# Joined entries and stage changes: tile order at three entries, the last weight slab of the delta layer, key squares, values and the first output tile

## The chip, the cores and the metric

The kernel runs on one core of a Trainium2 chip. The metric is the device time of one execution in microseconds (us), the median of the timed runs. Lower is better. TensorE is called PE here, VectorE DVE, ScalarE ACT, GpSimd POOL and SyncE SP.

## The reference

A block of three layers on 512 tokens of width 1024, all in float32: a bidirectional gated delta layer (8 heads) with its MLP, a bidirectional gated linear attention layer (4 heads) with its MLP, and a modulated layer with latent attention (4 heads, 256 context tokens ahead of the 512) beside four pooling groups.

```python
for i in range(2):
    m = _mixer_gdn(x, ...) if i == 0 else _mixer_gla(x, ...)
    x = _layernorm(DEEPNORM_ALPHA * x + m, ln1_g[i], ln1_b[i])
    x = _layernorm(DEEPNORM_ALPHA * x + _sq_relu_mlp(x, mlp_w1[i], mlp_w2[i]), ln2_g[i], ln2_b[i])
# second block
q, k, v = _mla_qkv(u, ...); kc, vc = ...      # q, k: rms-normed over 128 + 64 rotary columns
attn = _attend(q, concat(kc, k), concat(vc, v))
y = _branches(u, attn, w_pool, pool_scale) @ w_out
x = x + gate[:, None, :] * y
```

`_mixer_gdn` projects x to q, k, v, z and gates, convolves, and solves per head a triangular system in chunks; the kernel does that by doubling in levels.

## The kernel before

**Weights.** Every large product takes its weights in slabs of 1 MB (128 partitions x 2048 columns) through two raw halves. `load_slab` (L239, SP queue) fetches a half when the low part of the one before it is made. `split_hi` (L247, ACT) rounds a half to the high part `whi`, `split_lo` (L255, DVE) subtracts to the low part `wlo`, and `mm3` (L278, lines 280 to 282, PE) multiplies high by high, high by low and low by high. A slab is therefore two ACT and two DVE instructions of 1024 columns each. The semaphores `w_hi_ready` and `w_ready` count the halves in the order of the slabs, so the order of the splits is fixed while their place in each engine's program is free.

**Engines and order.** Each engine has its own program, written out by hand; engines meet only at semaphores. An instruction waits behind all that stand ahead of it on its own engine.

**The entries.** A token stage (a_out, down0, b_out) ends with x of 4 tiles of 128 tokens. `dve_token_end` (L487) adds and normalizes each tile (`dve_norm_tile` L431: sum, statistics, then after ACT's `act_norm_tile` two instructions, in two halves each for tile 3), PE turns it (`pe_turn_half`), ACT's `act_turned` makes its high parts `act_hi` and `dve_turned` (L416) its low parts `act_lo`, two halves for a tile. Before, DVE makes tile 1's low parts between tile 3's statistics and tile 3's norm. `pe_feature_first` (L1582) opens the next feature stage (up0, b_qk, up1): it needs tiles 0 and 1 to begin, multiplies them for output tiles 0 and 1 in groups of three matmuls of 256 columns, turns the two halves of tile 3 after the first and the second four groups of output tile 0, and goes on with tiles 2 and 3.

**The delta layer.** `pe_a_in` projects in 16 slabs. Behind the last one ACT and DVE split the second slab of a_out (`next_pair("a_in", 7)`, b = 1) and then begin the heads: a table load, `act_a_decays`, `act_a_decay(0)` (L1256), DVE's `dve_a_k` and `dve_a_first_pairs` (L1374, L1380), and PE's `pe_a_decay_turn` (L1023). Each of the 8 heads has levels l = 1 to 6, each with products (L1092), transposes (L1101), copies on ACT and products and additions on DVE (L1440, L1453).

**c_in and attention.** `pe_c_in` ends with head 0's keys, their sums, the query sums (L2608) and six value products (L2583), alternating between banks 6 and 7, read out by ACT (t = 0, 2, 4) and DVE (t = 1, 3, 5). ACT and DVE split the second slab of c_out ahead of these. `pe_c_attend` goes through 16 steps n, four query tiles for each of four heads. A step has the next tile's score (L2834, L2835, banks 0 to 3), pieces of the next head's preparation (key products L2600, query L2590, sums L2604, L2608, in bank 7), the value product of the step before (L2854, bank 6) and the transposes of the probabilities (L2843, banks 4 and 5). DVE's `dve_c_softmax`, `dve_c_max`, `dve_c_rope` (L2759) and `dve_c_keys` (L2764, L2765) belong to it; the last two scale the next head's key and rotary key by its norm, in the step with qt = 2. GpSimd adds the rotary squares and does the pooling beside it. At the end `act_c_mix` and `dve_mix` (L570, L574) split the mixed tiles and c_out begins.

## Time and profile before

| | |
|---|---|
| timed runs | median 1873.69 us (1873.48 to 1875.39, 3 runs) |
| profiled execution | 1872.41 us, its span 1870.4 us |
| PE busy | 1820.5 us, 97% of the span |
| DVE busy | 986.4 us, 53% |
| ACT busy | 733.7 us, 39% |
| POOL busy | 235.6 us, 13% |
| split_hi, one half (L253) | 1053 ns, 214 times |
| split_lo, one half (L259) | 1224 ns, 214 times |
| granted clock, mean | 0.993 of full speed |

Busy times are those of the profile's first part, the two splits those of its fifth. The span runs from the first to the last instruction; the rest of the execution lies around it. The granted clock is TensorE's; 1.00 is 2.4 GHz.

### The profile page before, as it was taken

The page shows a single profiled execution, that of the slowest core. Times are in us where ns is not written, and L with a number is a line of the kernel's source. Part 1 is how long each engine was busy: PE and PEld are TensorE (multiplying, and loading weights), DVE is VectorE, ACT ScalarE, POOL GpSimd, SP SyncE. Part 2 cuts the span into 40 slices and gives each one's busy share as a digit, 9 for nine tenths or more (in the row PEclk, how much of TensorE's full clock was granted, in tenths as well). Part 3 has the DMA queues.
Part 4 walks back from the last instruction along what each step waited for, and adds up shares of the span by engine and source line. Part 5 has one row for each costly group of instructions (what it writes and reads, how often), then busy time and mean ns, then how long its engine had stood idle before and what let it go on. Part 6 is the DMA issues. An engine that isn't in the chain of part 4 may idle for free.

```text
span 1870.4 us, 24188 instructions
## 1 busy us (share of the span) xinstructions
PE 1820.5 (97%) x9152; PEld 1471.2 (79%) x9152; DVE 986.4 (53%) x1393; ACT 733.7 (39%) x1209; POOL 235.6 (13%) x230
## 2 busy tenths in 40 slices
PE   8999999999999999999999999999999998999999
PEld 6887798888788888887777787888888887875667
DVE  5775466666554453356321577744443567323663
ACT  4344455554232232333443444222223355334340
POOL 2001234342000001000000253000000000201500
PEclk9999999999999999999999999999999999999999
DMA  5323100000342234222222200442235222421001
GB/s 157 90 90 112 46 2 1 1 1 1 122 148 90 90 90 149 90 90 90 68 91 68 68 1 23 129 164 90 90 112 180 90 90 79 149 70 45 1 1 68
DMA packets 102374, 146.77 MB, mean 78 GB/s; under 512 B 4977, under 2 KB 70721, under 8 KB 102032
## 3 DMA queue, kind: packets, MB, share of 16 engines
q1 hardware_dynamic: 95472, 121.45, 20.5%
q0 software_dynamic: 6816, 24.13, 3.9%
q8 instruction: 59, 0.97, 0.2%
q14 instruction: 27, 0.22, 0.0%
HBM read 143.47 MB, written 2.10 MB: 78 GB/s over the span
## 4 chain that ended last, share of the span: by engine, by line
PE 91%; DVE 3%; issue 2%; ACT 2%; POOL 1%; DMA 1%; SPq 0%; ACTq 0%; DVEq 0%; POOLq 0%
PE bk L280 23%; PE bk L282 23%; PE bk L281 23%; PE bk L1092 2%; PE bk L1110 2%; PE bk L2834 1%; PE bk L2835 1%; PE bk L1101 1%; PE bk L2854 1%; PE bk L990 1%; POOL work L1512 1%; PE bk L1973 1%; PE bk L1008 1%; PE bk L1121 1%; PE bk L1152 1%
## 5 line engine op out<-in xcount | busy, mean ns | idle before, releaser
L259 DVE TENSOR_TENSOR wlo<-raw,whi 128x1024 fp32r<-128x1024 f32 x214 | 253.4, 1224 | 376.9 <-ACT whi L253 373.2
L280 PE MATMUL bk<-act_hi,whi 128*128 128x512 f32 x960 | 384.0, 400 | 0.3 <-DVE wlo L723 0.3
L281 PE MATMUL bk<-act_lo,whi 128*128 128x512 f32 x960 | 380.6, 396 | 0.0
L282 PE MATMUL bk<-act_hi,wlo 128*128 128x512 f32 x960 | 380.5, 396 | 0.0
L253 ACT ACTIVATE whi<-raw 128x1024 fp32r<-128x1024 f32 x214 | 216.1, 1053 | 265.5 <-PE bk L282 248.8
L280 PE MATMUL bk<-whi,act_hi 128*128 128x512 f32 x768 | 308.6, 402 | 2.5 <-DVE act_lo L473 1.8
L281 PE MATMUL bk<-wlo,act_hi 128*128 128x512 f32 x768 | 304.8, 397 | 0.0
L282 PE MATMUL bk<-whi,act_lo 128*128 128x512 f32 x768 | 304.7, 397 | 0.0
L280 PEld LDWEIGHTS bk<-act_hi,whi 128*128 128x128 f32 x960 | 180.5, 188 | 48.9 <-issue 4.1
L282 PEld LDWEIGHTS bk<-act_hi,wlo 128*128 128x128 f32 x960 | 180.5, 188 | 44.5
L281 PEld LDWEIGHTS bk<-act_lo,whi 128*128 128x128 f32 x960 | 180.6, 188 | 44.4 <-issue 1.0
L280 PEld LDWEIGHTS bk<-whi,act_hi 128*128 128x128 f32 x768 | 145.5, 189 | 38.9 <-issue 3.1
L282 PEld LDWEIGHTS bk<-whi,act_lo 128*128 128x128 f32 x768 | 145.3, 189 | 36.1
L281 PEld LDWEIGHTS bk<-wlo,act_hi 128*128 128x128 f32 x768 | 145.4, 189 | 34.6 <-issue 0.5
L1633 DVE TENSOR_TENSOR arena<-arena (+1 forms) x64 | 44.3, 692 | 182.2 <-ACT arena L1616 182.2
L1616 ACT ACTIVATE arena<-bk 128x512 f32 (+1 forms) x64 | 38.3, 598 | 245.2 <-PE bk L282 245.2
L1942 POOL TENSOR_TENSOR work<-work,arena 128x512 f32<-128x512 f32 x24 | 37.5, 1583 | 381.3 <-ACT work L1926 355.5
L473 DVE TENSOR_TENSOR act_lo<-arena,act_hi 128x2048 fp32r<-128x2048 f32 x32 | 73.3, 2292 | 18.8 <-ACT act_hi L467 18.8
L829 DVE SCALAR_TENSOR_TENSOR work<-work,convw 128x512 f32<-128x512 f32 x96 | 64.6, 743 | 0.0
L467 ACT ACTIVATE act_hi<-arena 128x2048 fp32r (+1 forms) x32 | 60.9, 1904 | 6.3 <-PE bk L282 6.3
L1092 PE MATMUL bk<-work 128*128 128x128 f32 x384 | 61.1, 280 | 1.3 <-DVE work L1433 1.2
L1440 DVE TENSOR_TENSOR work<-bk,work 128x256 f32<-128x256 f32 x96 | 40.6, 424 | 36.5 <-PE bk L1092 34.9
(392 smaller groups left out, 2500.8 us busy)
## 6 DMA issues: line engine op xcount, KB each, us to landing
raw<-in_mlp_w SPq DMA_DIRECT2D x128, 512.0 KB, 4.2
raw<-in_a_w_in SPq DMA_DIRECT2D x32, 512.0 KB, 4.0
work<-in_w_mod POOLq DMA_DIRECT2D x24, 512.0 KB, 4.1
raw<-in_b_w_in SPq DMA_DIRECT2D x24, 512.0 KB, 3.8
raw<-in_w_in SPq DMA_DIRECT2D x14, 512.0 KB, 4.0
raw<-in_a_w_out SPq DMA_DIRECT2D x8, 512.0 KB, 4.2
raw<-in_b_w_out SPq DMA_DIRECT2D x8, 512.0 KB, 4.0
raw<-in_w_out SPq DMA_DIRECT2D x8, 512.0 KB, 3.9
```

Of the source, the lines that this page charges most:

```text
L253: nc.scalar.activation(whi[b][:, hs], raw[hf][:, :], ACT.Copy).then_inc(w_hi_ready, 1)
L259: nc.vector.tensor_tensor(wlo[b][:, hs], raw[hf][:, :], whi[b][:, hs], ALU.subtract).then_inc(w_ready, 1)
L280: nc.tensor.matmul(acc, lhs_hi, rhs_hi, start=first, stop=False, skip_group_check=True)
L281: nc.tensor.matmul(acc, lhs_hi, rhs_lo, start=False, stop=False, skip_group_check=True)
L282: return nc.tensor.matmul(acc, lhs_lo, rhs_hi, start=False, stop=last, skip_group_check=True)
L467: nc.scalar.activation(stage(act_hi, b), hid_group(pair, b), ACT.Copy).then_inc(stage_hi_ready, 1)
L473: nc.vector.tensor_tensor(stage(act_lo, b), hid_group(pair, b), stage(act_hi, b), ALU.subtract).then_inc(stage_ready, 1)
L829: nc.vector.scalar_tensor_tensor(out=acc, in0=src, scalar=wk, in1=acc, op0=ALU.mult, op1=ALU.add).then_inc(conv_step, 1)
L1092: mm = nc.tensor.matmul(bk[s][:, c % 2 * P:c % 2 * P + P], A["K"][:, c, :], z_right(l, c * P, P), start=True, stop=True, skip_group_check= ...
L1440: nc.vector.tensor_tensor(A["T"][:, 2 * s:2 * s + 2, :], chunks(bk[s])[:, 0:2, :], A["negpair"][:, l, :].unsqueeze(1).broadcast_to([P, 2, ...
L1616: nc.scalar.activation(head_tile(hid, k2 * 4, 2 * b + j), bk[2 * b + j][:, :], ACT.Relu).then_inc(acc_free, 1)
L1633: nc.vector.tensor_tensor(tile, tile, tile, ALU.mult).then_inc(hid_ready, 1)
```

## The change

- Entries: DVE makes tile 1's low parts ahead of tile 3's sum, and tile 2's low parts one half ahead of tile 3's norm and one behind it. ACT makes tile 2's high parts ahead of tile 3's statistics. PE turns the two halves of tile 3 after the first and second four groups of output tile 1.
- Delta layer: the last slab is split in the heads h = 1 and h = 2 (the second and third), one half in each, behind level 3.
- c_in: the six value products go to banks 2, 3, 6, 7, 4, 5, each with the wait for that bank's reader; the waits for their copies move behind the first score.
- Attention: the second slab of c_out is split one half at n = 3 and one at n = 7. Head 1's second key product goes to bank 6 and doesn't wait for the first one's square. The keys of the next head are scaled ahead of the softmax of qt = 2, their rotary part where it was.
- c_out: the first output tile's products of the first slab are issued ahead of the last value product.

```diff
-        def split_hi(act, k, b):
-            for hf in range(2):
+        def split_hi(act, k, b, parts=(0, 1)):
+            for hf in parts:
...
 act_token_end:
-            for st in range(1, ST):
+            for st in (1, 2):
                 act_norm_tile(act, e, st)
                 act_turned(act, e, [st - 1])
+            act_turned(act, e, [2])
+            act_norm_tile(act, e, 3)
             act_turned(act, e, [3])
 dve_token_end:
-            dve_norm_tile(dve, name, e, 3, lambda: dve_turned(dve, e, 1))
-            dve_turned(dve, e, 2)
+            dve_turned(dve, e, 1)
+            dve_norm_tile(dve, name, e, 3, lambda: dve_turned(dve, e, 2, (0,)))
+            dve_turned(dve, e, 2, (1,))
             dve_turned(dve, e, 3)
 pe_feature_first:
                 part(0, range(4 * hf, 4 * hf + 4), 0, 2)
+            for hf in range(2):
+                part(1, range(4 * hf, 4 * hf + 4), 0, 2)
                 pe_turn_half(pe, e, before, 3, hf)
-            part(1, range(0, 8), 0, 2)
 act_a_in (dve_a_in alike):
-                    split_hi(act, next_pair("a_in", k2), b)
+                    if (k2, b) != (7, 1):
+                        split_hi(act, next_pair("a_in", k2), b)
 act_a_head (dve_a_head alike):
+                if l == 3 and h in (1, 2):
+                    split_hi(act, next_pair("a_in", 7), 1, (h - 1,))
 pe_c_in:
-            pe.wait_ge(V.sem, V.at("qt", 0))
-            pe.wait_ge(K.sem, K.at("lnq", 0))
             for t in range(6):
-                if t in (2, 4):
-                    pe.wait_ge(K.sem, K.at("v", t // 2 - 1))
-                if t in (3, 5):
-                    pe.wait_ge(V.sem, V.at("v", t // 2 - 1))
-                T.inc(nc.tensor.matmul(bk[6 + t % 2][:, :]...
+                if t == 0:
+                    pe.wait_ge(acc_free, 2 * FS["c_in"] + 16)
+                elif t == 2:
+                    pe.wait_ge(V.sem, V.at("qt", 0))
+                elif t == 3:
+                    pe.wait_ge(K.sem, K.at("lnq", 0))
+                elif t == 4:
+                    pe.wait_ge(K.sem, K.at("lnk", 1))
+                T.inc(nc.tensor.matmul(bk[V_BANK[t]][:, :]...
-            pe.wait_ge(K.sem, K.at("v", 2))
-            pe.wait_ge(V.sem, V.at("v", 2))
+        V_BANK = (2, 3, 6, 7, 4, 5)
 act_c_in (dve_c_in alike):
-            split_hi(act, next_pair("c_in", 3), 1)
 pe_c_value:
+            elif qt == 0:
+                pe.wait_ge(K.sem, K.at("sqk", 3))
 pe_c_attend:
+                if n == 0:
+                    pe.wait_ge(K.sem, K.at("v", 0))
+                    pe.wait_ge(V.sem, V.at("v", 0))
                 if n + 1 < NB:
                     pe_c_score(pe, n + 1)
+                if n == 0:
+                    pe.wait_ge(K.sem, K.at("v", 2))
+                    pe.wait_ge(V.sem, V.at("v", 2))
...
                 if g < NH and qt == 0:
-                    pe.wait_ge(K.sem, K.at("sqk", 2 * g))
-                    pe_c_key(pe, g, 1, 7)
+                    if g == 1:
+                        pe_c_key(pe, g, 1, 6)
+                    else:
+                        pe.wait_ge(K.sem, K.at("sqk", 2 * g))
+                        pe_c_key(pe, g, 1, 7)
...
                 pe_c_transpose(pe, n)
+                if n == NB - 1:
+                    pe_token_slab(pe, "c_out", 0, 0, 0, 0, True, False, tiles=(0,))
 act_c_attend (dve_c_attend alike):
+                if n in (3, 7):
+                    split_hi(act, next_pair("c_in", 3), 1, (n // ST,))
 dve_c_attend:
+                if qt == 2 and g < NH:
+                    dve_c_key_scaled(dve, g)
                 dve_c_softmax(dve, n)
...
                 if qt == 2 and g < NH:
                     dve_c_rope(dve, g, 7)
-                    dve_c_keys(dve, g)
+                    dve_c_key_rope(dve, g)
```

## Rows read from the trace of the kernel before

**Rows 1.** Waits of PE: engine, line, waited for: us in total, times, longest.

```profile
PE bk L280 <- issue: 5.9, 3, 2.1
```

**Rows 2.** Timeline, up0's entry: start, us, engine, line, tiles, count [idle before <-releaser].

```profile
513.00 1.28 DVE L450 SCALAR_TENSOR_TENSOR X<-X,rstd,work 128x1024 f32<-128x1024 f32 x1
...
514.34 1.09 PE L395 MATMUL bk<-eye,X 128*128 128x128 f32 x8
...
515.91 1.23 DVE L420 TENSOR_TENSOR act_lo<-bk,act_hi 128x512 fp32r<-128x512 f32 x2
...
517.25 0.36 PE L280 MATMUL bk<-act_hi,first_hi 128*128 128x256 f32 x1 [1.82 <-issue]
...
518.75 0.60 PE L395 MATMUL bk<-eye,X 128*128 128x128 f32 x4
...
519.29 0.75 DVE L450 SCALAR_TENSOR_TENSOR X<-X,rstd,work 128x512 f32<-128x512 f32 x1
```

**Rows 3.** Timeline, from the last slab of a_in to the first head.

```profile
204.09 1.99 ACT L253 ACTIVATE whi<-raw 128x1024 fp32r<-128x1024 f32 x2
...
205.24 1.88 PE L1008 MATMUL bk<-work 128*128 128x512 f32 x4
206.10 1.28 ACT L744 ACT_TABLE_LOAD   x1
...
207.93 0.63 ACT L1256 ACTIVATE work<-bk 128x512 f32<-128x512 f32 x1
...
210.03 0.63 PE L1023 MATMUL bk<-eye,work 128*128 128x128 f32 x4 [2.47 <-DVE work L1380]
```

**Rows 4.** Timeline, second head behind level 3, and last head at its level 3.

```profile
251.44 0.87 DVE L1453 TENSOR_TENSOR work<-work,bk 128x256 f32<-128x256 f32 x2 [0.60 <-PE bk L1110]
...
253.68 0.42 DVE L1440 TENSOR_TENSOR work<-bk,work 128x256 f32<-128x256 f32 x1 [1.37 <-PE bk L1092]
...
444.22 1.06 DVE L574 TENSOR_TENSOR act_lo<-act_f,act_hi 128x512 fp32r<-128x512 f32 x1
```

**Rows 5.** Timeline of PE from the end of c_in to the first query tile.

```profile
1699.73 0.95 PE L2608 MATMUL bk<-ones,arena 128*128 128x2 f32 x8
...
1709.97 1.10 PE L2834 MATMUL bk<-work,arena 128*128 128x512 f32 x2 [0.83 <-issue]
...
1717.40 0.70 PE L2600 MATMUL bk<-arena,work 128*128 128x256 f32 x2 [1.18 <-ACT work L2636]
...
1718.85 1.98 PE L2590 MATMUL bk<-arena,work 128*128 128x512 f32 x4
...
1720.67 1.02 PE L2834 MATMUL bk<-work,arena 128*128 128x512 f32 x2
```

**Rows 6.** Timeline, first change of head in attention.

```profile
1732.36 1.57 DVE L2764 TENSOR_TENSOR work<-work 128x768 f32<-128x768 f32 x1
...
1733.86 2.01 DVE L2765 TENSOR_TENSOR work<-arena,work 128x768 f32<-128x768 f32 x1
...
1736.13 2.04 PE L2834 MATMUL bk<-work 128*128 128x512 f32 x2 [1.86 <-DVE work L2765]
...
1743.70 1.02 PE L2834 MATMUL bk<-work 128*128 128x512 f32 x2
```

**Rows 7.** Windows: us; busy of PE, PEld, DVE, ACT, POOL; clock; DMA share, GB/s.

```profile
1735.00:1740.00 5.00, 3.87 (x5) 1.83 (x6) 3.36 (x7) 0.80 (x3) 4.69 (x5) 0.52 0.00 0
...
1710.00:1820.00 110.00, 102.79 (x488) 70.40 (x489) 67.34 (x137) 50.30 (x123) 32.70 (x24) 0.97 0.00 1
```

**Rows 8.** Timeline, second and third change of head, and end of attention.

```profile
1766.98 1.10 PE L2834 MATMUL bk<-work,arena 128*128 128x512 f32 x2 [1.63 <-ACT arena L2918]
...
1771.63 1.02 PE L2834 MATMUL bk<-work,arena 128*128 128x512 f32 x2
...
1792.24 0.95 DVE L2765 TENSOR_TENSOR work<-arena,work 128x768 f32<-128x768 f32 x1
...
1819.49 1.60 PE L2854 MATMUL bk<-arena 128*128 128x128 f32 x12 [1.23 <-ACT arena L2918]
```

More of the change, by code:

```diff
@@ L305, in wait_tile, with pe_token_slab @@
                 eng.wait_ge(slab_used, k2 * 2 + (PH[name][0] + b + 1))
-        def pe_token_slab(pe, name, half, k2, b, pair0, first, last, after=None, order=range(ST)):
+        def pe_token_slab(pe, name, half, k2, b, pair0, first, last, after=None, order=range(ST), tiles=range(ST)):
             pe.wait_ge(w_ready, k2 * 4 + 2 * (PH[name][0] + 2 * pair0 + b + 1))
@@ L316, in pe_token_slab @@
             for i, st in enumerate(order):
+                if st not in tiles:
+                    continue
                 tok = slice(st * P, st * P + P)
@@ L414, in act_turned, with dve_turned @@
                                          ACT.Copy).then_inc(act_hi_ready, 1)
-        def dve_turned(dve, e, st):
-            for hf in range(2):
+        def dve_turned(dve, e, st, halves_of=(0, 1)):
+            for hf in halves_of:
                 dve.wait_ge(act_hi_ready, 8 * e + 2 * st + hf + 1)
@@ L843, in dve_a_in @@
                 for b in range(2):
-                    split_lo(dve, next_pair("a_in", k2), b)
+                    if (k2, b) != (7, 1):
+                        split_lo(dve, next_pair("a_in", k2), b)
                     if k2 == 7 and b == 0:
@@ L1457, in dve_a_head @@
                     dve_a_rows_low(dve)
+                if l == 3 and h in (1, 2):
+                    split_lo(dve, next_pair("a_in", 7), 1, (h - 1,))
                 if l == 3 and not more:
@@ L2711, in act_c_in @@
             act_c_query_norm(act, 0)
-            split_hi(act, next_pair("c_in", 3), 1)
             for t in (0, 2, 4):
                 act.wait_ge(T.sem, T.at("v", t))
-                K.inc(nc.scalar.activation(c_v[:, t, :], bk[6][:, :], ACT.Copy), "v")
+                K.inc(nc.scalar.activation(c_v[:, t, :], bk[V_BANK[t]][:, :], ACT.Copy), "v")
         def act_c_pin(act, b, j):
@@ L2746, in dve_c_in @@
             dve_c_rope(dve, 0, 6)
-            dve_c_keys(dve, 0)
+            dve_c_key_scaled(dve, 0)
+            dve_c_key_rope(dve, 0)
             dve_c_scale_column(dve, 0)
-            split_lo(dve, next_pair("c_in", 3), 1)
             for t in (1, 3, 5):
                 dve.wait_ge(T.sem, T.at("v", t))
-                V.inc(nc.vector.tensor_copy(c_v[:, t, :], bk[7][:, :]), "v")
+                V.inc(nc.vector.tensor_copy(c_v[:, t, :], bk[V_BANK[t]][:, :]), "v")
         def dve_c_rope(dve, g, bank):
@@ L2759, in dve_c_rope, with dve_c_key_scaled, dve_c_key_rope @@
             V.inc(nc.vector.tensor_tensor(HB[g % 2]["qt"], bk[bank][:, :], CW["tabq"], ALU.mult), "qt")
-        def dve_c_keys(dve, g):
+        def dve_c_key_scaled(dve, g):
             dve.wait_ge(K.sem, K.at("expk", g))
-            kn, kr = HC[g % 2]["kn"], HC[g % 2]["kr"]
+            kn = HC[g % 2]["kn"]
             V.inc(nc.vector.tensor_tensor(kn, kn, c_rsk, ALU.mult), "kn")
-            V.inc(nc.vector.tensor_tensor(kr, c_kr, c_rsk, ALU.mult), "kr")
+        def dve_c_key_rope(dve, g):
+            V.inc(nc.vector.tensor_tensor(HC[g % 2]["kr"], c_kr, c_rsk, ALU.mult), "kr")
         def dve_c_scale_column(dve, g):
@@ L2934, in act_c_attend @@
                     for half in range(2):
-                        act_c_key(act, g, half, 7)
+                        act_c_key(act, g, half, 6 if (g, half) == (1, 1) else 7)
                 elif qt == 1:
@@ L3014, in dve_c_attend @@
                 dve_c_turned(dve, n)
+                if n in (3, 7):
+                    split_lo(dve, next_pair("c_in", 3), 1, (n // ST,))
                 if qt == 2 and g < NH:
@@ L3159, in _ @@
                 for b in range(2):
-                    pe_token_slab(pe, "c_out", half, 0, b, half, b == 0, b == 1)
+                    pe_token_slab(pe, "c_out", half, 0, b, half, b == 0, b == 1, tiles=range(half == 0 and b == 0, ST))
 _INS = ["x", "a_w_in", "a_conv", "a_alog", "a_dt_bias", "a_norm_g", "a_w_out", "b_w_in", "b_gate_w2", "b_gate_b",
```

4 lines of the change are left out of this document (2 added, 2 removed).

## The prediction

> **What bounds the kernel now.** The page's first part comes first: TensorE (PE) is busy for 97% of the span (the table above), VectorE (DVE) for 53% and ScalarE (ACT) for 39%. No edit removes a matmul, so what can be won is PE's idle time, some 50 us of 1870.4, and the time that PE spends at its lower clock. The second view is therefore the waits of PE. Its second largest entry is 5.9 us in three waits [rows 1], one at each of the three entries into a feature stage. The third view, the timeline around each wait in the edited functions, says what ends it. The profiled execution took 1872.41 us, of which 1870.4 are the span; the timed runs have their median at 1873.69, 1.28 us above. I work out a difference against the profiled execution and subtract it from the median.
>
> **The three entries (into up0, b_qk, up1).** At 514.34 PE turns tile 2 into banks (1.09 us, so until 515.43) and then waits for tile 1's low parts: two DVE instructions that start at 515.91, last 1.23 us and release PE at 517.25 [rows 2]. They stand that late because DVE first takes tile 3's sum and statistics. DVE's instruction ahead of those, the end of tile 2's norm, starts at 513.00 and takes 1.28 us. With the new order tile 1's low parts run from about 514.2 to 515.45, and PE, which now starts 0.11 us after their end, starts at about 515.56. That is 1.69 us of the 1.82 idle there; 0.13 us stay. The three waits together are 5.9 us, so 5.5 us go.
> What is late next is tile 3. Its sum waits behind 1.23 us of DVE and the first half of its norm behind one low part of tile 2 (0.62), where two (1.23) stood. The last instruction of its norm (519.29, 0.75 us [rows 2]) then ends at about 520.5 instead of 520.04, while PE is 1.7 us earlier: 2.2 us of margin are used. PE meets this by the new order of its parts. The first four groups on tiles 0 and 1 take it from 517.25 to the first half turn at 518.75, 1.5 us with a restart [rows 2]; it now does 16 such groups, 5.8 us, before the second half turn of tile 3, where it did 8. With the first half turn that is 515.56 + 6.1, about 521.7, and the norm is done at 520.5. The low part of tile 3's first half is ready near 521.7 too, and PE wants it 0.35 us later. I take no new wait; bounds 0 to 0.5 us for each entry.
>
> **Last slab of the delta layer.** ACT's two high splits from 204.09 (1.99 us) are followed by a table load (206.10, 1.28 us) and the decays (to 207.93); the exponential at 207.93 feeds DVE and then PE, which restarts at 210.03 after 2.47 us of idle [rows 3]. Without the splits the table load ends near 205.5 and the decays near 206.1, but the exponential also needs PE's decay sums, which start at 205.24 and take 1.88 us, to 207.12. It starts near 207.15, 0.8 us earlier, and the two DVE instructions behind it follow. So of the 2 us taken off ACT 0.8 count; bounds 0.3 to 1.0.
> The splits come back in the second and third head, one ACT instruction (1.05 us) and one DVE (1.22 us, the table above) each. In the second head the level-3 additions of DVE end at 252.31 and its next product starts at 253.68 [rows 4]: a hole of 1.37 us in which 1.22 fit. ACT waits for the same additions there. GpSimd works beside them, and then a DVE instruction with two SBUF inputs gets longer: at the same place of the last head one of 512 columns takes 1.06 us [rows 4]. The split has 1024; at twice 1.06 it ends at 254.4 and DVE is 0.75 us late, in a level whose results PE wants after two more transposes and a 512-column sum. I take 0; upper bound 0.7 us for each of the two heads.
>
> **The values at the end of c_in.** Before, PE goes from the query sums at 1699.73 (0.95 us) to the first score at 1709.97 [rows 5]. Between them are six products of 512 columns, two passes each. Four such passes take from 1718.85 to 1720.67 with a restart [rows 5], 0.43 each without it, so the six products need 5.2 us. The rest is waiting for two banks to be read by engines that hold 2 us of splits in front. Now six banks are used and the splits are gone: the products run from 1700.68 to 1705.9 and the score starts there, its keys being long ready. That is 4.1 us; lower bound 3.0 (one bank still read late), upper 4.2.
> Head 1's second key product waits 1.18 us, until 1717.40, for ACT to square the first half out of the same bank, and the query product stands at 1718.85, 8.88 us after the first score [rows 5]. In bank 6 the key product follows at once. But the query product needs both squares. ACT's first square is ready 7.4 us after the score as before, and the two reads of the second half follow it directly, 0.6 to 0.7 us, where a product and its latency stood ahead of them. So the query product starts at 8.1, 0.8 us earlier, and in front of it a new wait of about 0.9 us appears.
>
> **The three changes of head.** At 1732.36 DVE scales the keys (1.57 us) and then their rotary part (2.01), and PE starts the next head's score at 1736.13 after 1.86 us of idle [rows 6]. The first scaling now stands ahead of the softmax, where DVE is idle. The rotary part then runs from 1732.4; its length lies between 0.95 (no GpSimd work beside it [rows 8]) and 2.01, and it ends at 1733.3 to 1734.4. PE, free at 1734.3, starts at 1734.3 to 1734.6: 1.5 to 1.86 us, taken 1.7. The second change, 1.63 us of idle [rows 8], gives 1.3 to 1.63 in the same way, taken 1.6. At the third GpSimd is still and little is waited for: 0.2. Sum 3.5.
> Beside the first change the granted clock falls: 0.52 of full speed from 1735 to 1740 [rows 7], the lower level, 1.2 GHz. Ahead of it PE did the query sums (8 products of 2 columns), six transposes and the idle. From score to score PE then takes 1736.13 to 1743.70, 7.57 us [rows 6], and for the same sequence at full clock, at the second change, 1766.98 to 1771.63, 4.65 [rows 8]. With the idle gone I expect the clock to stay up: 2.9 us.
>
> **The split inside attention, and the last tile.** One half of the slab is split at n = 3 and one at n = 7. DVE's 1.22 us come ahead of the next softmax, whose result PE needs only after a score, two key products and a value product, some 5 us; the softmax and its maximum fill about 3 of them. Cost 0; with that cover gone, at most 1.2 each.
> The Trainium skill ("SBUF — State Buffer", Who interferes with whom) speaks against these places: DVE and GpSimd share a port pair, a DVE instruction with two SBUF inputs waits for a GpSimd instruction under way to end, and the other way round. The lengthened key scalings [rows 6] agree with it; what it would make of the splits is rival 3.
> At the end PE idles 1.23 us in front of the last value product at 1819.49 [rows 8], since ACT copies six mixed tiles ahead of the turned probabilities. The 12 matmuls of the first output tile now stand there. They need DVE's fourth mixed tile, which is under way at that time, so I take about half, 0.7 us; bounds 0 and 1.2.
>
> **The sum.** 5.5 + 0.8 + 4.1 + 0.8 + 3.5 + 2.9 + 0.7 = 18.3 us. 1873.69 - 18.3 = 1855.4.
>
> **The rivals.**
> 1. *The clock gives nothing.* The fall may not be in the timed runs at all, or come back elsewhere. Against: all quiet stretches of PE in the edited places get shorter. Gain 15.4, time 1858.3. Its mirror: the timed runs, which lie above the profiled one, have one more fall that goes too: 1852.5.
> 2. *Tile 3 bounds the entries*, and the wait only moves behind the first parts: 1860.9. For it: the margin of 0.35 us comes out of several overlapped starts. Against: an error of 0.5 us costs 0.5, and losing all takes tile 3 about 2 us later than worked out.
> 3. *The splits stall PE.* If GpSimd lengthens each of the four DVE halves by the 1.06 us that the rotary scaling lost (2.01 against 0.95 [rows 6, 8]) and none of it is covered, 4.2 us go: 1859.6.
> 4. *Slower.* DVE becomes the bound of attention. Place: the 16 query tiles, 110 us, in which DVE is busy for 67.34 [rows 7]: 4.2 us of 6.9 a tile. It decides from 2.7 us more a tile on, 43 us in all; the splits and their lengthening add 2.4 to 4.6. For it speaks only that GpSimd's 33 us lie beside. If each tile came 1.4 us late, 22 us would be paid: 1877.
> 5. *The change doesn't do what it says*: the values wait for something unseen in the new banks, the clock falls anyway and the entries wait for tile 3; what is left is under 0.2%.
>
> **How the numbers follow.** My forecast 0.60; rival 1 0.15, its mirror 0.05; rival 2 0.09; rival 3 0.07; rival 4 0.02; rival 5 0.02. The range from 1851.5 to 1861 holds the forecast, rivals 1 to 3 and the bounds of the unknown costs (up to 1.5 for the entries, 1.4 for the heads, 1.1 for the values). What a measurement of this kernel tells from no change is about 0.2%, or 3.7 us: faster by more 0.96, within 0.02, slower 0.02.
>
> **What would show it.** In the profile after: the three waits in front of the first feature product under 0.3 us; the restart in the delta layer after some 1.7 us in place of 2.47; no wait between the six value products, and the first score about 6.2 us after the query sums begin; a new wait near 0.9 us in front of head 1's query product; a clock of 1.00 over all of attention; the first output tile ahead of the last value product. I am wrong if PE waits for tile 3's low parts in the entries, if it waits for DVE's level products in the second and third head of the delta layer, or for the softmax of n = 4 or n = 8.

## The result, and the profile after

| | before | after |
|---|---|---|
| timed side by side, 4 runs each | median 1874.45 us (1873.48 to 1875.39) | median 1849.39 us (1848.04 to 1854.21) |
| ratio | | 0.9871, 95% interval 0.9852 to 0.989 |
| profiled execution (span) | 1872.41 us (1870.4) | 1854.21 us (1852.2) |
| mean granted clock of the profiled execution | 0.993 | 0.994 |
| mean granted clock of the other three timed runs | not listed | 0.998, 0.997, 0.998 |

The kernel became 25 us faster, between 21 and 28 by the interval. The forecast was 18.3 us and 1855.4 us; the measured median lies 6.0 us below it and 2.1 us below the range. The profiled execution of after, however, is 18.2 us shorter than that of before, in time and in span. So the question is not only what the change does, but why two profiled executions differ by 18 us and the medians by more.

The page of after, first part. Busy time of PE fell by 4 us, that of the others hardly moved, and the number of matmuls is the same.

```profile
PE 1816.4 (98%) x9152; PEld 1471.9 (79%) x9152; DVE 988.1 (53%) x1393; ACT 734.7 (40%) x1209; POOL 237.2 (13%) x230
```

The waits of PE, in the form of [rows 1]. The three waits that made 5.9 us make 0.5 us together. The restart of the delta layer waits 1.7 us. New are a wait of 0.64 us in front of head 1's query product and one of 0.49 in front of the first output tile; both stand in brackets in the rows further down. The largest of those that the last stage keeps is its first product's, 4.2 us (4.1 before).

```profile
PE bk L280 <- DVE act_lo L2408: 4.2, 1, 4.2
...
PE bk L1030 <- DVE work L1389: 1.7, 1, 1.7
...
PE bk L280 <- issue: 0.5, 3, 0.2
```

up0's entry, DVE's timeline and then PE's first feature product, against [rows 2]. Tile 1's low parts follow tile 2's norm at once and PE starts 0.10 us behind their end, with 0.15 us of idle. Tile 3's norm ends at 520.75, 0.71 us later than before, and no row of PE waits for it.

```profile
513.21 1.28 DVE L452 SCALAR_TENSOR_TENSOR X<-X,rstd,work 128x1024 f32<-128x1024 f32 x1
514.41 1.28 DVE L422 TENSOR_TENSOR act_lo<-bk,act_hi 128x512 fp32r<-128x512 f32 x2
...
520.00 0.75 DVE L452 SCALAR_TENSOR_TENSOR X<-X,rstd,work 128x512 f32<-128x512 f32 x1
```

```profile
515.79 0.36 PE L280 MATMUL bk<-act_hi,first_hi 128*128 128x256 f32 x1 [0.15 <-issue]
```

The delta layer, against [rows 3 and 4]. The table load starts 1.97 us earlier, the exponential only 0.85, since it needs PE's sums. In the second head DVE's half of the split takes 1.59 us beside GpSimd, and the level product behind it starts at 254.09, 1.52 us after the split began.

```profile
204.13 1.28 ACT L749 ACT_TABLE_LOAD   x1
...
207.08 0.60 ACT L1263 ACTIVATE work<-bk 128x512 f32<-128x512 f32 x1 [0.98 <-PE bk L1015]
```

```profile
209.14 0.63 PE L1030 MATMUL bk<-eye,work 128*128 128x128 f32 x4 [1.66 <-DVE work L1389]
```

```profile
252.57 1.59 DVE L259 TENSOR_TENSOR wlo<-raw,whi 128x1024 fp32r<-128x1024 f32 x1
254.09 0.41 DVE L1449 TENSOR_TENSOR work<-bk,work 128x256 f32<-128x256 f32 x1
```

PE from the end of c_in to the second tile's score, against [rows 5]. The twelve passes of the values stand without a gap, the first score 6.05 us behind the start of the query sums (before 10.24), the query product 7.90 behind the score (before 8.88).

```profile
1694.51 0.95 PE L2622 MATMUL bk<-ones,arena 128*128 128x2 f32 x8
1695.32 5.40 PE L2597 MATMUL bk<-work,arena 128*128 128x512 f32 x12
1700.56 1.02 PE L2849 MATMUL bk<-work,arena 128*128 128x512 f32 x2
...
1708.46 1.98 PE L2604 MATMUL bk<-arena,work 128*128 128x512 f32 x4 [0.64 <-ACT work L2650]
```

The first change of head, against [rows 6]: the keys scaled early, the rotary part 1.57 us, the score without a wait at 1723.82; and behind it the split, 1.75 us on DVE.

```profile
1716.99 0.96 DVE L2777 TENSOR_TENSOR work<-work 128x768 f32<-128x768 f32 x1 [0.21 <-ACT work L2661]
...
1721.98 1.57 DVE L2780 TENSOR_TENSOR work<-arena,work 128x768 f32<-128x768 f32 x1
...
1729.01 1.75 DVE L259 TENSOR_TENSOR wlo<-raw,whi 128x1024 fp32r<-128x1024 f32 x1
```

```profile
1723.82 1.10 PE L2849 MATMUL bk<-work 128*128 128x512 f32 x2
```

The end of attention, against [rows 8]: the wait of 1.23 us is gone, the output tile starts after 0.49.

```profile
1801.37 0.47 PE L280 MATMUL bk<-whi,act_hi 128*128 128x512 f32 x1 [0.49 <-DVE act_lo L579]
```

Last the windows, with the columns of [rows 7]; the clock stands behind the busy times. Attention is at 1.00. But four stretches elsewhere are at 0.50, that is 1.2 GHz: in the first delta head, behind the modulation's small products in down0 and down1, and behind the 4.2 us wait at the start of the last stage. The first of the four is not in the profiled execution of before. It does not come from the change: the kernel before with products in the changes of head (further down), which is the kernel before up to 1730 us, has it too, from 211 us on.

```profile
212.00:214.00 2.00, 2.00 (x12) 2.00 (x11) 0.85 (x2) 1.09 (x3) 2.00 (x3) 0.50 0.00 0
700.00:704.00 4.00, 4.00 (x13) 3.42 (x14) 3.25 (x3) 1.22 (x1) 2.39 (x4) 0.50 0.70 198
1387.00:1390.00 3.00, 3.00 (x9) 2.42 (x9) 2.65 (x4) 0.25 (x1) 1.42 (x2) 0.50 0.87 261
1580.00:1583.00 3.00, 3.00 (x16) 3.00 (x16) 2.27 (x6) 3.00 (x8) 0.00 (x0) 0.50 0.38 86
1700.00:1820.00 120.00, 117.81 (x572) 83.93 (x571) 75.97 (x145) 55.31 (x129) 32.34 (x24) 1.00 0.05 15
```

### The profile page after: what moved, and what is told of

The parts are those of the page before. It is cut to its first block, busy times and chain, and to the rows that moved or that the text cites. A ratio compares the mean times of both kernels' runs of the same rounds, so it can differ in the third digit from the quotient of the medians.

```text
span 1852.2 us, 24189 instructions
## 1 busy us (share of the span) xinstructions
PE 1816.4 (98%) x9152; PEld 1471.9 (79%) x9152; DVE 988.1 (53%) x1393; ACT 734.7 (40%) x1209; POOL 237.2 (13%) x230
## 4 chain that ended last, share of the span: by engine, by line
PE 93%; DVE 2%; issue 2%; ACT 2%; POOL 1%; DMA 1%; SPq 0%; ACTq 0%; DVEq 0%; POOLq 0%
PE bk L280 23%; PE bk L281 23%; PE bk L282 23%; PE bk L1099 2%; PE bk L1117 2%; PE bk L1108 1%; PE bk L2849 1%; PE bk L2850 1%; PE bk L2871 1%; PE bk L1015 1%; PE bk L997 1%; POOL work L1523 1%; PE bk L1985 1%; PE bk L1128 1%; PE bk L1159 1%
## 5 line engine op out<-in xcount | busy, mean ns | idle before, releaser
L1099 PEld LDWEIGHTS bk<-work 128*128 128x128 f32 x384 | 52.8, 192 | 9.6 <-issue 6.0
```

The costliest lines, as they stand in the source:

```text
L1099: mm = nc.tensor.matmul(bk[s][:, c % 2 * P:c % 2 * P + P], A["K"][:, c, :], z_right(l, c * P, P), start=True, stop=True, skip_group_check= ...
```

## The experiments

Two theories stood against each other. One: the mechanisms are those of the forecast, and the rest is TensorE's clock, which falls at different quiet stretches in different executions, so that one profiled execution does not show what the median holds. The other: some part of the change is worth more than was worked out. All kernels were timed in turn with the kernel before.

**The changed kernel again.** No edit.

> The changed kernel itself, for the spread of its runs with their clocks. Theory (clock): the single runs differ only by how much of each was spent at TensorE's lower clock; 0.001 of mean granted clock goes with about 1.8 us (half of 0.2% of 1848), single runs between 1847 and 1855, median near 1849.5. Rival (profiling or chance): runs of the same clock differ as much, and time and mean clock don't go together.

Measured 1852.60 us (1847.89 to 1854.35, 5 runs), ratio 0.9889 [0.9868, 0.991]. The five runs lie in order of their clock: 0.994, 0.994, 0.995, 0.996 and 0.998 go with 1854.35, 1854.23, 1852.60, 1851.51 and 1847.89 us. A line through the nine runs of both series has a slope of 1.5 us per 0.001 of mean clock, with 0.3 us of scatter about it. The nine have their median at 1851.51. The kernel before, in the 59 runs of all series, has its median at 1873.44 (1866.02 to 1879.79), and the 55 whose clock is listed (0.989 to 0.997) lie on the same slope, with 1.2 us of scatter. So the difference of these medians is 21.9 us, where the first four runs, three of them at a high clock, gave 24.3 against the 1873.69 that the forecast started from. Of the 6.0 us by which it was off, 2.4 are that, the draw of four runs; the other 3.6 have to be explained. The 21.9 are not sharp themselves: in samples drawn anew from these runs the difference lies between 18 and 25 us in 95 of 100. Runs at the same clock compare better: with one slope for both kernels they lie 17.3 us apart. The mean clocks are 0.9932 and 0.9960, and this difference is worth 4 us by the slope.

The Trainium skill ("TensorE: Matmul & The Clock Gate", Terms) puts the penalty of the gate at the throttled time times one half. An estimate by it is 1.9 us for 0.001 of mean clock over 1870 us. The runs give 1.5, and the measurement decides.

**Only the entries.** The kernel before with the new order at the three entries.

```diff
@@ the three entries: ScalarE, VectorE, TensorE
+            act_turned(act, e, [2])
+            act_norm_tile(act, e, 3)
...
+            dve_turned(dve, e, 1)
+            dve_norm_tile(dve, name, e, 3, lambda: dve_turned(dve, e, 2, (0,)))
+            dve_turned(dve, e, 2, (1,))
...
+            for hf in range(2):
+                part(1, range(4 * hf, 4 * hf + 4), 0, 2)
+                pe_turn_half(pe, e, before, 3, hf)
```

> The kernel before with the new order of the three entries alone. Theory (terms as worked out): 5.5 us faster than the kernel before, near 1869. Theory (clock): in timed runs the quiet stretch of each entry, a tile turn and an idle of 2 us, sometimes brought a fall as well, so 6 to 10 us faster, and a higher mean clock than before. Rival (tile 3 bounds): under 3 us.

Measured 1864.92 us (1858.29 to 1868.3, 12 runs), ratio 0.9955 [0.9942, 0.9968]: 8.4 us, between 6.0 and 10.9. The idle time that goes is 5.5. More goes here than the idle time, and the interval excludes 5.5. The mean clock of the runs is 0.9944 where before has 0.9932, which is worth 1.7 us by the slope.

**Products in the quiet stretches of the changes of head.** The kernel before with extra products; its waits stay.

```diff
@@ pe_c_score
+            if qt == 0 and h > 0:
+                pe.wait_ge(w_ready, 2 * (PH["c_out"][0] + 1))
+                for _ in range(6):
+                    nc.tensor.matmul(bk[0][:, :], whi[0][:, 0:P], whi[0][:, 0:512], start=True, stop=True, skip_group_check=True)
```

> The kernel before, with six products of 512 columns more (1.4 us, their result overwritten) ahead of the score at each of the three changes of head in attention; the waits stay. Theory (clock): the fall at the first change doesn't happen, 2.9 us less in the profile, and in the timed runs 2 to 5 us less where there are falls at the first two changes; the third change, with little idle, costs 1.2 us more. Net 1 to 4 us faster than before. Rival (the clock gives nothing in timed runs): 1.2 us slower than before.

Measured 1872.02 us (1869.4 to 1874.31, 12 runs), ratio 0.9998 [0.9986, 1.0011]. In the profile attention keeps its full clock. But the windows show a lower clock right behind each of the three entries, where the profiled execution of before has 1.00, and none behind the modulation, where that one has it:

```profile
518.00:520.00 2.00, 1.81 (x9) 1.84 (x10) 1.97 (x4) 0.38 (x1) 0.00 (x0) 0.59 0.51 201
890.50:892.50 2.00, 2.00 (x12) 2.00 (x11) 1.97 (x4) 0.00 (x0) 0.00 (x0) 0.50 0.03 8
1208.00:1210.00 2.00, 2.00 (x9) 2.00 (x10) 1.94 (x3) 0.15 (x1) 0.08 (x1) 0.50 0.48 197
698.00:704.00 6.00, 6.00 (x43) 5.45 (x41) 4.34 (x5) 3.62 (x5) 0.00 (x0) 1.00 0.01 3
1730.00:1740.00 10.00, 9.56 (x53) 7.18 (x52) 9.12 (x15) 2.37 (x8) 9.26 (x8) 1.00 0.00 0
```

Up to 1730 this kernel is the kernel before, instruction for instruction. So the same code falls at the entries in one execution and in down0 in another. The forecast of 1 to 4 us is not borne out. What the filling of the head changes is worth can't be told from this run: the products cost 1.1 us of their own at the third change (shown further down), and the interval is 5 us wide.

**Products in the quiet stretches of the entries.** The kernel before, its three waits kept, with six products of 512 columns in each.

```diff
@@ the entries' products of PE
+            pe.wait_ge(w_ready, 2 * PH[name][0] + 1)
+            for _ in range(6):
+                nc.tensor.matmul(bk[0][:, :], first_hi[:, 0:P], first_hi[:, 0:512], start=True, stop=True, skip_group_check=True)
             pe.wait_ge(act_ready, 8 * e + 4)
```

> The kernel before, with six extra matmuls of 512 columns (into a bank that holds nothing then) put into TensorE's quiet stretch at each of the three entries; all waits there stay, so no idle time is removed as work and nothing is computed faster. Theory A (part of the entries' gain is clock: in some executions the granted clock falls beside the entries' quiet stretches, 3.4 us at the lower level at each, which costs 1.6 us each): the median lies 2 to 4 us under the kernel before, about 1870.5, although the three waits are only filled. Rival B (the entries are worth their idle time alone and the 8.5 us that the entries gave in the medians have another source): within 1 us of the kernel before, 1873 to 1874.5. Rival C: the extra products come late and cost time, 1 to 3 us over it.

Measured 1868.41 us (1865.61 to 1873.43, 12 runs), ratio 0.9976 [0.9963, 0.999]: 4.5 us, between 1.9 and 6.9, without one instruction of the real work earlier. PE still waits at each entry for the same low parts:

```profile
518.97 0.39 PE L280 MATMUL bk<-act_hi,first_hi 128*128 128x256 f32 x1 [0.59 <-DVE act_lo L420]
```

This is theory A: the entries of the kernel before cost idle time and, on top of it, clock. The size is loose; the mean clock of these runs (0.9955 against 0.9932) gives 3.3 us by the slope. In its profiled execution no lower clock follows the second modulation block or the first change of head either, which this edit leaves alone (1.00 from 1387 to 1395 and from 1735 to 1742 us). So the run shows a gain in clock without any gain in idle time, but not that all of it was lost behind the entries. The forecast had no such term.

**Key scaling late.** The changed kernel with `dve_c_key_scaled` back beside the rotary part.

```diff
@@ dve attention loop
-                if qt == 2 and g < NH:
-                    dve_c_key_scaled(dve, g)
                 dve_c_softmax(dve, n)
...
                     dve_c_rope(dve, g, 7)
+                    dve_c_key_scaled(dve, g)
                     dve_c_key_rope(dve, g)
```

> The changed kernel with the key scaling back beside the rotary one, behind the softmax, at the three changes of head. By the terms as worked out the waits of 1.86, 1.63 and 0.17 us come back: 3.5 us slower than the changed kernel. Theory (clock): in part of the runs a fall at one or both of the first two comes with it, 1.5 to 3 us each, so 4 to 9 us slower in the median and a wider spread. Rival: 3.5 us and no more, with the mean clock unchanged.

Measured 1856.19 us (1852.59 to 1859.97, 6 runs), ratio 0.9912 [0.9892, 0.9932], 4.7 us above the changed kernel's nine runs; that lies between the rival's 3.5 and the clock's 4 to 9, and with six runs it decides neither. Both waits of before are back, with the durations of [rows 6 and 8]:

```profile
PE bk L2849 <- DVE work L2780: 1.9, 1, 1.9
PE bk L2849 <- ACT arena L2946: 1.6, 1, 1.6
```

In its profiled execution the fall behind the first change is back too, where the changed kernel has 1.00:

```profile
1724.00:1727.00 3.00, 3.00 (x7) 1.70 (x6) 1.77 (x2) 0.00 (x0) 2.84 (x3) 0.50 0.00 0
```

From score to score there PE takes 6.33 us (1722.86 to 1729.19), against the 4.65 of full clock: 1.7 us.

**The modulation's products spread.** The changed kernel keeps, as before did, a block of 32 products of two columns (4.5 us) ahead of down0 and of down1, behind which its clock is at 0.50. Here a quarter of the block follows each of the four token tiles of the slab behind it.

```diff
@@ pe_mod, and the first slab of down0 and down1
-            for n in range(8):
-                for w in range(2):
...
+        def mod_part(third):
+            def after(pe, st):
+                for n in (2 * st, 2 * st + 1):
+                    for w in range(2):
...
```

> The changed kernel, with the block of 32 two-column matmuls of the modulation (4.34 us, after which both profiles show a clock fall of 6.8 us, near 699 and 1385 us) spread in eight parts over the following slab, four small products behind each token tile's products. Theory A (falls of the clock follow whatever quiet stretch is left, and this block is the one that both kernels keep): no fall near 699 and 1385 in the profile, 3 to 6 us faster than the changed kernel, about 1846. Rival B (the falls come at intervals whatever PE does, and only move): 0 to 1 us from the changed kernel, mean granted clock as there. The small products themselves take as long in either place.

Measured 1849.64 us (1849.07 to 1850.3, 4 runs), ratio 0.9879 [0.9854, 0.9904]. The clock of its runs is 0.998 to 0.999, the fall near 1580 (here from 1574 us) alone is left in the profile while PE has work, and the runs lie within 1.3 us where the changed kernel's nine span 6.5. But only 1.9 us are won on the median of the nine, not 3 to 6, because the block had hidden something: without it PE waits 0.69 us for ScalarE's last copies of the layer ahead, in both places.

```profile
696.96 0.50 PE L280 MATMUL bk<-whi,act_hi 128*128 128x512 f32 x1 [0.69 <-ACT arena L1629]
...
699.86 0.95 PE L1695 MATMUL bk<-ones,work 128*128 128x2 f32 x8
```

**Filled.** The same, with products also in the two longest waits of PE that are left and that it can fill.

```diff
@@ start of the last stage (4.2 us) and of the first delta head (1.7 us)
+            for _ in range(14):
+                nc.tensor.matmul(bk[0][:, :], first_hi[:, 0:P], first_hi[:, 0:512], start=True, stop=True, skip_group_check=True)
...
+            for _ in range(5):
+                nc.tensor.matmul(bk[0][:, :], whi[0][:, 0:P], whi[0][:, 0:512], start=True, stop=True, skip_group_check=True)
```

> The changed kernel with the modulation's block spread as in the kernel above, and with extra 512-column products in the two longest waits that are left: 14 in the wait of 4.15 us at the start of the last stage, 5 in the wait at the first head of the delta layer. The waits stay, only the engine is busy in them. Theory A (the clock is what spreads the runs): mean granted clock 0.998 or more in the profile, no fall near 211 and 1580, median 1 to 3 us under the kernel with the spread alone (1844 to 1846), and a spread of the runs under 3 us where the changed kernel had 6.5. Rival B: the falls move elsewhere, the median is that of the kernel above or higher by the filler's own cost (up to 1 us), the spread stays at 6 us.

Measured 1847.39 us (1847.16 to 1847.59, 4 runs), ratio 0.9865 [0.9841, 0.989]. All four runs have a mean clock of 1.000, and they lie within 0.43 us. The last fall of the profile starts at 1844 us, behind PE's last product, and costs nothing. The stretches that were at 0.50 in the changed kernel:

```profile
212.00:214.00 2.00, 2.00 (x17) 1.81 (x16) 1.31 (x4) 1.58 (x5) 2.00 (x3) 1.00 0.00 0
698.00:704.00 6.00, 6.00 (x36) 5.15 (x34) 4.10 (x3) 2.16 (x2) 0.00 (x0) 1.00 0.52 171
...
1575.00:1580.00 5.00, 5.00 (x46) 5.00 (x45) 4.17 (x10) 5.00 (x13) 0.00 (x0) 1.00 0.37 105
```

That shows the second half of the first theory: what spreads the runs of this kernel is the clock, and with the quiet stretches filled it does not fall while PE works. The median is 1.4 us above the forecast of 1844 to 1846, by the same two waits. This kernel is also a ruler: on it a part can be sized to half a microsecond.

**The kernel before, filled in the same way.** It gets the three aids above and the products at the entries and the changes of head; nothing of the change is in it, and its waits stay.

```diff
@@ before
+ the edits of: modulation's products spread, filled, products in the entries, products in the changes of head
```

> The kernel before with the same aids as the filled kernel (modulation's products spread, extra 512-column products in the waits at the start of the last stage and of the first delta head) and also with extra products in its own quiet stretches at the three entries and the three changes of head. All waits of before stay, so nothing of the change is in it; the clock should have no cause to fall. Theory A (the change is worth its idle time, and what the medians show beyond that is the clock): mean granted clock 0.998 or more, median 1862.5 to 1864.5, that is 15 to 17 us over the filled changed kernel (1847.4), the forecast without its clock term being 15.4; about 9 us under the kernel before, all of it clock. Rival B (the kernel before is slower for another reason than idle time and clock): 1866 or more at that clock.

Measured 1864.28 us (1863.9 to 1865.3, 10 runs), ratio 0.9959 [0.9947, 0.9972], clock 0.999 to 1.000. Against the filled kernel that is 16.9 us at the same clock. Of these 1.1 are no loss of the kernel before: at the third change of head hardly any wait was there to fill, and the six products push the score.

```profile
1783.37 0.85 PE L2862 MATMUL bk<-eye,work 128*128 128x128 f32 x6
1783.98 1.64 PE L2845 MATMUL bk<-whi 128*128 128x512 f32 x6
1785.46 1.02 PE L2853 MATMUL bk<-work 128*128 128x512 f32 x2
```

From the transposes to the score it is 2.09 us here, and in the kernel before, by the same two rows of its timeline, 1.02:

```profile
1792.43 0.85 PE L2843 MATMUL bk<-eye,work 128*128 128x128 f32 x6
1793.45 1.10 PE L2834 MATMUL bk<-work 128*128 128x512 f32 x2 [0.17 <-issue]
```

What is left, 15.8 us, is the change without its clock, to within about 1 us: the two kernels were timed in different series, and the kernel before, brought to full clock by the slope, is 0.7 us faster in this series than in that of the filled kernel, which would make it 16.5. The forecast without its clock term was 15.4.

**The splits in front of the values again.** The changed kernel with the last slab's second half split where it stood before.

```diff
@@ ScalarE and VectorE ahead of the copies of the values
+            split_hi(act, next_pair("c_in", 3), 1)
+            split_lo(dve, next_pair("c_in", 3), 1)
@@ ScalarE and VectorE in attention
-                if n in (3, 7):
-                    split_hi(act, next_pair("c_in", 3), 1, (n // ST,))
-                    split_lo(dve, next_pair("c_in", 3), 1, (n // ST,))
```

> The changed kernel with one edit undone: the second slab of the output product is split ahead of the values of the last stage again (2 us of ScalarE and about 2.4 us of VectorE in front of the copies of the values), instead of inside attention at tiles 3 and 7. Theory A: the six products now have a bank each, so they still run without a wait; the copies come 2 to 2.5 us later, and the first value product and the key product of head 1 wait for them: 0.5 to 2 us slower than the changed kernel. Rival B (the six banks alone carried the 4.1 us of this term, the place of the splits nothing): within 0.5 us of the changed kernel. Rival C (the splits inside attention cost something there): 0.5 to 2 us faster.

Measured 1850.70 us (1848.35 to 1851.47, 4 runs), ratio 0.9885 [0.986, 0.991]. Rival B is right and theory A fell. The copies do start behind 2.35 us of splits, but the value passes still stand without a gap, and head 1's query product waits the same 0.64 us for the same square:

```profile
1691.99 2.35 DVE L259 TENSOR_TENSOR wlo<-raw,whi 128x1024 fp32r<-128x1024 f32 x2
1694.26 1.88 DVE L2767 COPY arena<-bk 128x512 f32<-128x512 f32 x3
```

```profile
1689.43 5.40 PE L2597 MATMUL bk<-work,arena 128*128 128x512 f32 x12
...
1702.58 1.98 PE L2604 MATMUL bk<-arena,work 128*128 128x512 f32 x4 [0.64 <-ACT work L2650]
```

By the slope, too, its runs lie 0.1 us from the changed kernel's at the same clock. So the six banks alone carry the term of the values. The place of the splits is free in both positions, in attention too.

**The first output tile last.** The filled kernel with the tile behind the last value product.

```diff
@@ pe_c_attend
-                if n == NB - 1:
-                    pe_token_slab(pe, "c_out", 0, 0, 0, 0, True, False, tiles=(0,))
```

> The filled changed kernel (1847.4, its four runs within 0.4 us) with the first output tile put back behind the last value product. Theory A: the idle of 1.2 us in front of the last value product returns, the half us in front of the output tile goes: 0.7 us slower, 1848.1. Rival B (another wait takes its place): no difference. 5 rounds on this base can tell 0.3 us apart.

Measured 1848.32 us (1847.86 to 1849.62, 5 runs), 0.9 us over the filled kernel; ratio to before 0.9876 [0.9855, 0.9897]. The wait of [rows 8] is back at its old length. From the first score to the last matmul the two profiled executions differ by 0.76 us.

```profile
1794.94 1.27 PE L2883 MATMUL bk<-arena 128*128 128x128 f32 x9 [1.23 <-ACT arena L2956]
```

**PE's old order at the entries.** The filled kernel with the half turns of tile 3 among tile 0's parts; VectorE and ScalarE keep the new order.

```diff
@@ the entries' products of PE
                 part(0, range(4 * hf, 4 * hf + 4), 0, 2)
-            for hf in range(2):
-                part(1, range(4 * hf, 4 * hf + 4), 0, 2)
                 pe_turn_half(pe, e, before, 3, hf)
+            part(1, range(0, 8), 0, 2)
```

> The filled changed kernel with TensorE's old order of parts at the three entries (half turns of tile 3 among tile 0's parts), the new order of VectorE and ScalarE kept. Theory A (of the prediction: tile 3's norm is now later, and the old order would wait for it): a wait of 2 to 3.5 us in front of tile 3's first half turn at each entry, in all 6 to 10 us slower, 1853.5 to 1857.5. Rival B (the margin was never needed): under 1 us in all. The part of it that shows as clock rather than idle is up to 1.7 us an entry.

Measured 1855.44 us (1853.82 to 1856.66, 6 runs), ratio 0.9911 [0.9891, 0.993]: 8.1 us over the filled kernel. PE waits in front of the half turn for tile 3's norm, 5.7 us in three waits, as much as the old waits in front of the first product:

```profile
518.36 0.66 PE L398 MATMUL bk<-eye,X 128*128 128x128 f32 x4 [1.90 <-DVE X L453]
```

The last 2.4 of the 8.1 us are no idle time of these rows. The runs' clock is 0.998 to 1.000 where the filled kernel's is 1.000 throughout, which by 1.5 us per 0.001 gives 1.2 to 1.5 of them. In the profiled execution the clock falls right behind the second of the three waits:

```profile
890.00:893.00 3.00, 3.00 (x17) 3.00 (x16) 1.91 (x3) 0.60 (x1) 0.00 (x0) 0.51 0.02 5
```

**A quarter of each block in front.** The filled kernel with the modulation's first eight products back ahead of the slab, where they cover the 0.69 us wait.

```diff
@@ pe_mod
+            mod_part(pe, -1)
             pe.wait_ge(acc_free, 2 * FS[name] + 32)
```

> The filled changed kernel with the first quarter of each modulation block back in front of the slab (it hid ScalarE's last copies, for which TensorE now waits 0.7 us twice) and only the other three quarters spread behind tiles 0 to 2. Theory A: the two waits of 0.7 us go and the clock stays up, 1846.0, the fastest of all. Rival B: eight small products are enough to let the clock fall: 1848 or more, runs spread over some us again.

Measured 1845.53 us (1845.18 to 1846.12, 4 runs), ratio 0.986 [0.9836, 0.9885], clock 1.000 in all four. It is the fastest of all: 1.9 us under the filled kernel (of another series, see above; the two waits of 0.69 us account for 1.4) and 6.0 under the nine runs of the changed one. The extra products do nothing but keep PE busy.

## Why the prediction was wrong, step by step

The mechanisms of the sum hold; the step that failed is the term for the clock. It was too small. The prediction put it as "With the idle gone I expect the clock to stay up: 2.9 us", for the first change of head alone, since that was the one fall beside an edited place that the profiled execution of before showed [rows 7]. The runs show 4 to 6 us in its place, since the clock falls behind other quiet stretches too that the change removes. The work was put 0.4 to 1.9 us too low besides, depending on how it is measured, and 2.4 us are the draw of the first four runs. With the parts as the table has them, the 6.0 us by which the forecast was off are 0.9 of work, 2.7 of clock and 2.4 of draw.

| step | forecast | measured | from |
|---|---|---|---|
| entries, idle | 5.5 | 5.4 | waits 5.9 to 0.5 |
| delta layer, last slab | 0.8 | 0.9 | restart 210.03 to 209.14 |
| values | 4.1 | 4.2 | sums to score 10.24 to 6.05 |
| head 1's key product | 0.8 | 1.0 | score to query product 8.88 to 7.90 |
| output tile | 0.7 | 0.8 | first output tile last, in the span |
| changes of head | 3.5 | 4.0 | last tile's score of a head to the next head's first |
| change without clock, in all | 15.4 | 16.3 | the six parts above |
| the same | 15.4 | 15.8 | both kernels filled |
| the same | 15.4 | 17.3 | runs at the same clock |
| clock | 2.9 | 5.6, 6.1 | medians 21.9, less 16.3 or 15.8 |
| clock | 2.9 | 4 | mean clocks, by the slope |

*Changes of head.* Before, a head's last score and the next head's first lie 7.79, 7.56 and 6.10 us apart (from 1728.34, 1759.42 and 1787.35). After it is 5.86, 5.83 and 5.77 (from 1717.96, 1744.18 and 1770.37). That is 1.93, 1.73 and 0.33 us, each a little more than the wait that went, 1.86, 1.63 and 0.17, and the first two above their bounds. The row of before that starts the first of these stretches, then that of after; their ends stand in [rows 6] and in the result:

```profile
1728.34 1.02 PE L2834 MATMUL bk<-work,arena 128*128 128x512 f32 x2
```

```profile
1717.96 1.02 PE L2849 MATMUL bk<-work,arena 128*128 128x512 f32 x2
```

*The entries.* Right in size and in what came next: tile 3's norm is done at 520.75, and it costs nothing only because PE's parts were put in a new order with it. With the old order the gain in idle time is paid back in full, 5.7 us. That was rival 2's mechanism; it is real, and it is PE's new order of its parts that keeps it away.

*Delta layer.* Right. The second head's DVE half lay between the bounds, 1.59 us, and its level product starts 0.06 us after where it would have (253.68 before, and this kernel runs 0.35 us later there).

*Values.* Right in size, half wrong in the reason. "Now six banks are used and the splits are gone": the banks do it alone.

*The new wait* in front of head 1's query product was forecast at 0.9 us and is 0.64.

*The splits in attention.* The row shows 1.75 us for one half and no wait of PE behind it; rival 3's 4.2 us are nowhere. By the Trainium skill ("SBUF — State Buffer", Who interferes with whom) DVE and GpSimd hold their common port pair in turn. The trace agrees as to the length, 1.75 and 1.59 us against a mean of 1.23. That one waits until the other has ended is not seen in it: in the second head GpSimd's row (253.04, 2.03 us) starts inside DVE's, as far as the rough spans of GpSimd tell. The profile shows that the length is covered.

*The clock.* In this change of head the term was right: the clock stays up, and the 2.9 us of [rows 6 and 8] come back. They are in the 18.2 us between the two profiled executions. Against them stands a fall that only the profiled execution of after has, in the first delta head. From the restart of the layer to the same eight products it takes 6.52 us there and 5.31 in the filled kernel; that is 1.2 us. The rows of after and then of the filled kernel:

```profile
209.14 0.63 PE L1030 MATMUL bk<-eye,work 128*128 128x128 f32 x4 [1.66 <-DVE work L1389]
...
215.66 0.53 PE L1117 MATMUL bk<-work 128*128 128x128 f32 x3
```

```profile
209.10 0.63 PE L1034 MATMUL bk<-eye,work 128*128 128x128 f32 x4 [0.52 <-DVE work L1393]
...
214.41 1.35 PE L1121 MATMUL bk<-work 128*128 128x128 f32 x8
```

So the agreement of the two profiled executions with the sum, 18.2 and 18.3 us, is in part luck: 16.3 of work and 2.9 of clock come to 19.2, and the fall of 1.2, which unchanged code shows too in another execution, takes them down to 18.0. The sum was then taken off a median in whose runs the falls lie in other places: behind the entries too. Filling the entries alone gives 4.5 us (1.9 to 6.9), and taking their waits away gives 8.4 where 5.4 are idle. The mirror of rival 1 ("the timed runs have one more fall that goes too") had a chance of 0.05 and came nearest. Its two falls make 5.8 us of clock and 21.2 in all, close to the 21.9 of the medians of all runs; it named no place for the second fall. That the entries were among PE's longest quiet stretches in edited code, up to 2.1 us each and as long as the one beside the fall, stood in [rows 1 and 2], and was read as idle time only.

What stays open is the exact size of the clock's part, 4 by the slope and about 6 by the medians, and how it divides between entries and changes of head. The two runs that fill one of them alone have intervals of 5 us. Nor was it tried why the kernel before filled at the changes of head has its falls at the entries in its profiled execution; only that both places occur is shown.

## What to carry to other kernels

A TensorE-bound kernel's quiet stretches have two prices: their idle time, and the lower clock that follows in some of the executions. One profiled execution shows that clock in one set of places. Price every quiet stretch that an edit removes, and compare mean clocks before comparing medians. A kernel with its waits filled by idle products is a ruler that tells parts of a microsecond apart where plain runs spread over 6 to 14, and filling and spreading together were worth 6 us here. Before a block is moved, look for what it hides: each of these two blocks of 32 small products hid a wait of 0.7 us.

## What the runs showed of the hardware

- The mean granted clock explains most of the spread between runs: 1.5 us for each 0.001, with 0.3 us of scatter about the line in the changed kernel's nine runs and 1.2 in 55 of the kernel before. Filled, the changed kernel's clock is 1.000 and its runs lie within 0.43 us; unfilled, the kernel before spans 1866.02 to 1879.79 us in 59 runs.
- A block of 32 products of two columns counts as busy time of PE in the profile (4.51 us) and often has a clock of 0.50 behind it: 12 times of 16, over the eight profiled executions of kernels that have the two blocks. The exceptions are both blocks with the changes of head filled, the second with the entries filled and the first with the splits in front. Eight of them between 512-column products (0.95 us) have not, in all six profiled executions of kernels that spread them.
- In one execution the lower clock follows each of the entries' waits of 1.8 to 2.1 us, in another, of the same instructions up to there, none of them.
